# Latent attention: the query units of all eight token tiles first, then all value units, in place of one loop over both

## The reference, cut to what matters

```
def mla_attention(c_q, c_kv, k_rope, positions, q_norm_g, kv_norm_g, w_uq, w_ukv):
    q = (rmsnorm_2(c_q, q_norm_g) @ w_uq).reshape(B, S, MLA_HEADS, MLA_QK_DIM)          # 8 heads x 96
    q = jnp.concatenate([q[..., :MLA_NOPE_DIM], rope(q[..., MLA_NOPE_DIM:], positions)], axis=-1)
    q = q * (MLA_QK_DIM ** -0.5)
    kv = (rmsnorm_2(c_kv, kv_norm_g) @ w_ukv).reshape(B, S, MLA_HEADS, MLA_NOPE_DIM + MLA_V_DIM)
    k_nope, v = kv[..., :MLA_NOPE_DIM], kv[..., MLA_NOPE_DIM:]                           # 64 and 64 a head
    k_pe = rope(k_rope[:, :, None, :], positions)
    k = jnp.concatenate([k_nope, jnp.broadcast_to(k_pe, (B, S, MLA_HEADS, MLA_ROPE_DIM))], axis=-1)
    ...
        s = jnp.einsum('bqhd,bkhd->bhqk', q_blk, k).astype(jnp.float32)
        p = jax.nn.softmax(s, axis=-1).astype(v.dtype)
        return jnp.einsum('bhqk,bkhd->bqhd', p, v)
```

## Time and profile before

| | before |
|---|---|
| runs (median; lowest, highest) | 1961.69 us; 1956.64, 1961.73 |
| span of the profiled execution | 1955.4 us |
| median of the runs less that span | 6.3 us |
| PE busy | 1805.7 us (92%) |
| DVE, ACT, POOL busy | 869.1, 580.1, 470.5 us |
| mean granted TensorE clock | 0.964 |
| tile loop, first matmul to last value matmul | 1468.08 to about 1492.2 us |
| first matmul of the second key unit | 1496.52 us |

### The profile page before, as it was taken

How to read it: one execution, slowest core, us unless ns; L and a number is a source line. 1 busy time by engine, 2 the same in 40 slices (tenths; PEclk the granted TensorE clock), 3 DMA queues, 4 the chain that set the end, 5 groups by cost and what they waited for, 6 DMA issues and landing times. The chain is left out here.

```text
span 1955.4 us, 23181 instructions
## 1 busy us (share of the span) xinstructions
PE 1805.7 (92%) x9240; PEld 1540.5 (79%) x9240; DVE 869.1 (44%) x1393; ACT 580.1 (30%) x1320; POOL 470.5 (24%) x314
## 2 busy tenths in 40 slices
PE   4999899897999999999899999999997999968998
PEld 3777798676877768889898998877776888856776
DVE  4140577336502125521455305422325999963633
ACT  4101244124300114410243003411123776641111
POOL 5223300323322220202202121203321323230330
PEclk8999999898999999999999999999997999988999
DMA  6112200333322110101102011244443111124332
GB/s 195 28 65 66 64 1 1 114 121 114 102 86 70 44 44 17 60 12 44 45 21 61 19 42 44 66 139 134 135 159 113 30 33 31 25 92 145 124 119 86
DMA packets 85387, 142.44 MB, mean 73 GB/s; under 512 B 26656, under 2 KB 36512, under 8 KB 85152
## 3 DMA queue, kind: packets, MB, share of 16 engines
q10 hardware_dynamic: 55216, 84.46, 12.7%
q1 hardware_dynamic: 30064, 56.50, 9.7%
HBM read 102.20 MB, written 38.73 MB: 72 GB/s over the span
## 5 line engine op out<-in xcount | busy, mean ns | idle before, releaser
L495 POOL TENSOR_SCALAR w_hi<-w_stage 128x1024 fp32r<-128x1024 f32 (+4 forms) x123 | 129.2, 1054 | 1203.0 <-PEq L767 523.3
L499 POOL TENSOR_TENSOR w_lo<-w_stage,w_hi 128x1024 fp32r<-128x1024 f32 (+4 forms) x123 | 270.8, 2206 | 9.2
L762 PE MATMUL ps<-w_hi,h2T_hi 128*128 128x512 f32 x584 | 250.9, 430 | 2.3 <-issue 1.6
L762 PE MATMUL ps<-w_hi,h2T_lo 128*128 128x512 f32 x584 | 238.2, 408 | 0.0
L762 PE MATMUL ps<-w_lo,h2T_hi 128*128 128x512 f32 x584 | 237.9, 407 | 0.0
L1720 DVE TENSOR_TENSOR rope_cos_part<-ps,cos_dil 128x512 f32<-128x512 f32 x48 | 33.2, 692 | 374.7 <-PE ps L762 374.7
L762 PEld LDWEIGHTS ps<-w_hi,h2T_hi 128*128 128x128 f32 x584 | 161.2, 276 | 15.7 <-issue 5.1
L762 PEld LDWEIGHTS ps<-w_hi,h2T_lo 128*128 128x128 f32 x584 | 161.3, 276 | 10.5
L762 PEld LDWEIGHTS ps<-w_lo,h2T_hi 128*128 128x128 f32 x584 | 162.2, 278 | 9.3
L520 PE MATMUL ps<-h2T_hi,w_hi 128*128 128x512 f32 x384 | 156.0, 406 | 3.8 <-ACT gate_tiles L1207 2.4
L520 PE MATMUL ps<-h2T_lo,w_hi 128*128 128x512 f32 x384 | 153.9, 401 | 0.0
(11 more groups left out here) (265 smaller groups left out, 3583.5 us busy)
## 6 DMA issues: line engine op xcount, KB each, us to landing
w_stage<-in_w_in SPq DMA_DIRECT2D x76, 512.0 KB, 3.6
w_stage<-in_w_out SPq DMA_DIRECT2D x16, 512.0 KB, 3.6
gate_scr<-gate_tiles ACTq DMA_DIRECT2D x16, 512.0 KB, 2.9
gates<-gate_scr ACTq DMA_DIRECT2D x32, 256.0 KB, 2.7
dil_scr<-dil_out ACTq DMA_DIRECT2D x24, 264.0 KB, 2.1
dil_nums<-dil_scr ACTq DMA_DIRECT2D x24, 256.0 KB, 3.6
x_tiles<-in_x ACTq DMA_DIRECT2D x8, 512.0 KB, 8.7
x_back<-in_x ACTq DMA_DIRECT2D x8, 512.0 KB, 3.6
```

The lines of the kernel that those rows point to most:

```text
L495: last = nc.gpsimd.tensor_scalar(hi_, raw_, 1.0, 0.0, ALU.mult, ALU.add)
L499: last = nc.gpsimd.tensor_tensor(lo_, raw_, hi_.bitcast(F32), ALU.subtract)
L762: m = pe.matmul(ps[:, u % 2, :], toks(a, k), b[:, s, k, :], start=(k == 0 and b is wh and a is h2h), stop=(k == KT - 1 and a is h2l))
```

## The change

The loop over tiles is written as two on TensorE and on VectorE, and as three pieces on ScalarE: all query units with their spills, the last spill, then all value copies. Nothing is added or taken away: 96 query matmuls, 48 value matmuls, 16 query copies, 8 value copies, 8 ropes, 8 low parts and 8 spills as before, with the same waits between the same pieces. The buffers stay as they are.

```
 # TensorE
                 three_passes(ps[:, u % 4, 0:384], [ ... ]).then_inc(sem("qm_done"), 1)
+        for t in range(TT):
             if t >= 2:
                 pe.wait_ge(*after("vm_lo", t - 1))
             for n in range(2):
...
 # ScalarE
                                ACT.Copy, scale=float(MLA_QK) ** -0.5).then_inc(sem("qm_read"), 1)
-            act.wait_ge(*after("vm_done", t + 1))
-            act.activation(V2[:, t, :, 0, :], ps[:, 4 + t % 2, :].rearrange("p (h c) -> p h c", c=HD), ACT.Copy).then_inc(sem("vm_hi"), 1)
             if t >= 1:
                 act.wait_ge(*after("qm_roped", t))
                 act.dma_start(qm_d[P * (t - 1):P * t, :], q_sb[:, (t - 1) % 2].rearrange("p h c -> p (h c)")).then_inc(sem(f"qm_spill{(t - 1) % 2}"), 16)
+        act.wait_ge(*after("qm_roped", TT))
+        act.dma_start(qm_d[P * (TT - 1):, :], q_sb[:, (TT - 1) % 2].rearrange("p h c -> p (h c)")).then_inc(sem(f"qm_spill{(TT - 1) % 2}"), 16)
+        for t in range(TT):
+            act.wait_ge(*after("vm_done", t + 1))
+            act.activation(V2[:, t, :, 0, :], ps[:, 4 + t % 2, :].rearrange("p (h c) -> p h c", c=HD), ACT.Copy).then_inc(sem("vm_hi"), 1)
         for b in range(4):
             act.wait_ge(*after(f"g_spill{b}", 16 * 6))
-        act.wait_ge(*after("qm_roped", TT))
-        act.dma_start(qm_d[P * (TT - 1):, :], q_sb[:, (TT - 1) % 2].rearrange("p h c -> p (h c)")).then_inc(sem(f"qm_spill{(TT - 1) % 2}"), 16)
...
 # VectorE
             nc.vector.tensor_tensor(q_hi, q_t[:, 2], q_t[:, 3], ALU.add).then_inc(sem("qm_roped"), 1)
+        for t in range(TT):
             dve.wait_ge(*after("vm_hi", t + 1))
             nc.vector.tensor_tensor(V2[:, t, :, 1, :], ps[:, 4 + t % 2, :].rearrange("p (h c) -> p h c", c=HD),
```

## The result

The changed kernel takes 1969.50 us in the median of seven runs (1961.07 to 1976.24), beside 1959.72 for seven runs of the kernel before (1953.44 to 1962.06). The ratio is 1.0052, with a 95% interval from 1.0033 to 1.0071: slower by 10 us, between 6.5 and 14. It was predicted as 1969.1, slower by 7.4.

A forecast was written before the change was run, and what follows sets the result against it. The query spill loop and TensorE were taken to run side by side at 2.79 us a tile. Second key unit 8.1 us later, less 0.7 for its full clock, gave 7.4 on 1961.7: 1969.1 us, range 1963 to 1973.5.

The forecast's parts named there:

- The likeliest case: Tile loops: spill-paced queries, TensorE empty, two-bank value rounds, uncovered first key unit; 7.4 us slower, chance 0.55.
- Step 1, the pace: Query units: spill loop sets the pace, spills 2.4 and 2.9 us apart by turns, each issued 0.01 behind copies.
- the other end, 0.40: Query spills: issue 0.40 us behind the next tile's copies, pace stays 2.79, last spill only 0.9 us earlier.
- Step 1, the first spill: Tile 0's spill: issued at about 1474.6 where before it waited until 1475.49 behind the value copy.
- Step 2: Value units: TensorE without work for 6 us, then two-bank rounds of 2.9 us at half or 2.3 at full clock.
- Step 3: Way into head 0: nothing covers the first key unit; second key unit starts 8.1 us later, stage 7.4 slower.
- the 0.7 us that the second key unit was to give back: Second key unit: at full clock it takes 0.97 us in place of 1.66, returning 0.7.
- Half clock through all the value units: Rival, value units: half clock to their end, +10.0 us, 1971.7; chance 0.25 shared with later spill issue.
- the later issue: Rival, query spills: 0.40 us issue delay on top of half clock, +10.9 us, 1972.6; within the shared chance 0.25.
- the clock pays back: Rival, head 0: full clock from 1498 to 1512 cuts the loss to +2.4 us, 1964.1; chance 0.12.
- A stretch after 1512 that differs by more than a microsecond: Sign of being wrong, after the stage: a difference of over a microsecond beyond the shift.
- the queries run at TensorE's own pace: Rival, query units: 2.08 us a tile, last spill 4.1 us earlier, +3.3 us, 1965.0; chance 0.05.

The follow-up runs named there:

- e7_before_load: Kernel before, old order, with eight-tile room in `q_tok` and head 0's query load issued between the two key copies: ratio 1.0007 against the kernel before.
- e4_warm: Changed kernel with 44 idle matmuls into an unused bank between value units 1 and 2: ratio 1.0031 against the kernel before.
- e1_banks: Changed kernel with the eight value units spread over seven banks in place of two: ratio 0.9999 against the kernel before.
- e5_early_load: Changed kernel with head 0's query load issued between the value copies of tiles 2 and 3: ratio 1.0030 against the kernel before.
- e2_slots: Changed kernel with room for eight query tiles in `q_tok` in place of two: ratio 1.0020 against the kernel before.
- e6_before_slots: Kernel before, old order, with room for eight query tiles in `q_tok` in place of two: ratio 0.9993 against the kernel before.
- e8_combined: Changed kernel with eight-tile `q_tok`, seven value banks, and first key unit, its copies, last spill and head 0's load moved: ratio 0.9963 against the kernel before.

## Why the prediction was right, and where its terms were off

**The way it went.** The likeliest case was the one that came: spill loop, empty TensorE, rounds over two banks, and a key unit that nothing covers. The stage lost 8.95 us where the sum had 7.4. By its steps, in us from the first query matmul:

- **Step 1, the pace.** Spills were to be 2.4 and 2.9 apart by turns; behind the first they are 2.4 and 2.8. The choice of 0.01 for the issue behind the copies was right (0.05 to 0.07 measured); the other end, 0.40, is excluded by these rows. The Trainium skill's "Perfetto Trace Analysis", "Sequencer Loop", has the sequencer hand an engine instruction to a queue and go on to the next; the trace agrees for one waiting copy (0.05 us).
- **Step 1, the first spill.** This is the first term that was mis-sized, by 0.77. It was to land 2.31 after its issue and took 3.08. That puts tile 2's copies 0.7 late and, through the turns of the loop, the last spill 0.5 (25.46 for 24.9). For the same reason TensorE's waits for copies begin with tile 4 and not with tile 6. The first two spills, from issue to landing:

```profile
1477.60 3.08 DMA qmla_scr<-q_tok
...
1480.81 2.31 DMA qmla_scr<-q_tok
```

What else the DMA engines moved meanwhile is in the list of queues (packets, MB, share of the 16 engines). In the changed kernel, from 1477.6 to 1480.7:

```profile
q10 hardware_dynamic: 144, 0.39, 33.3%
q8 instruction: 1, 0.02, 2.1%
q1 hardware_dynamic: 17, 0.02, 1.7%
```

And before, from 1475.5 to 1477.8:

```profile
q10 hardware_dynamic: 144, 0.39, 43.9%
```

Queue 10 is the spill, 16 times nine packets. Queue 1 is SP's, with the weights of the output projection; its last packet ends 0.28 us after the issue, and the spill's first starts 0.83 after it, so the weights were out of the way. Queue 8 is one packet of 16 KB of the program's own instructions. It takes about 1 us, and behind it the last packets of the spill run one after another, 0.12 us apart, when all the others have ended. I read this as one engine that comes late by that packet; the spill lands with its last. The packets of other runs say the same (us from the spill's issue; the first column of numbers is the issue itself, from the first query matmul):

| kernel | issued | instruction packet | last packet of the spill | landed |
|---|---|---|---|---|
| before | 7.41 | -0.71 to 0.23 | 1.96 | 2.31 |
| e7_before_load | 7.22 | -0.75 to 0.52 | 1.97 | 2.33 |
| changed | 6.49 | 0.23 to 1.26 | 2.58 | 3.08 |
| e4_warm | 6.48 | 0.46 to 1.38 | 2.71 | 3.18 |
| e1_banks | 6.06 | 0.67 to 1.59 | 2.91 | 3.39 |
| e5_early_load | 6.83 | 0.66 to 2.13 | 3.46 | 3.93 |

In the last four the spill's last packet comes 1.32 to 1.33 us after the end of the instruction packet. In e5_early_load the weights had ended before the issue, and it was the slowest. In these runs the instruction packet starts 6.5 to 7.5 us into the stage, with either order. So the earlier issue won nothing, because it ran into a transfer that it had been behind. I had not asked what the earlier spill would meet. No run takes the packet away or moves it, so this rests on the times of the packets.
- **Step 2.** TensorE was to stand for 6 us and stood for 5.5. The rounds were taken as 2.9 and 2.3 and are 3.06 at half clock and 2.4 to 2.6 at full clock; value unit 7 ended 7.7 us after unit 2's start, where I had 7.4. The first matmul after a wait takes 0.1 to 0.2 longer than the next ones. The clock was back about 3.5 us after work began again (1498.32 to some 1501.8), where I had chosen 4.
- **Step 3.** From the first key unit to the second 2.44, as at full clock (2.5 with the drain in front of it). But the 0.7 us that the second key unit was to give back did not come: it ran at half clock, 1.61 us. The clock fell near 1508.7, just after a wait of 1.48 us, with gaps of up to 0.33 us between the value units before it. This is the second term that was mis-sized. I had counted on full clock because of the work before, and hadn't put the wait beside it. In e4_warm the same unit ran at full clock after the same 1.48 us, in e2_slots at half; what decides it stays open.

In sum, the first spill is 0.5 at the last spill, the value rounds 0.3 and the key unit 0.7, together 1.5; 8.95 less 7.4 is 1.55.

**The rivals.** Half clock through all the value units did not happen, nor did the later issue. That the clock pays back is excluded the other way: head 0 started at half clock in both kernels. In the changed one it lasted until after 1529, so that the fourth query tile's scores came 10.6 us after the first and not 8.5. That is the 2 us lost inside head 0. A stretch after 1512 that differs by more than a microsecond was a sign that I had named for being wrong, and it came. But the order doesn't decide it: the same stretch takes 10.4 and 10.5 us in e6_before_slots and e7_before_load, which have the old order, and 8.5 in e4_warm and e8_combined, which have the new one. It is about 8.5 or a little over 10 with either order, by one profile of each kernel; whether the new order makes the longer one more frequent isn't shown. That the queries run at TensorE's own pace is excluded by e2_slots: they do only when the spills are out of the way.

**The size.** The time was met by 0.4 us, which is luck in part: the runs of before had a lower median this time (1959.7 for 1961.7), and the slowdown was larger by as much. The chances leaned on a forecast that lay only 1.5 us beyond what can be told from no change; a forecast of the 8.95 us that the stage lost would have lain 3 us beyond.

## What to carry to other kernels

When two loops of equal pace run side by side, splitting one out saves nothing until the other's limit is lifted too: give the loop that stays its buffers and the one that moves its banks before reordering, and then move up what the new order lets go early. Without that last step the order broke even here. With two buffers, a unit waits for nothing only if its round through the engines is no longer than the time from one unit to the next but one: here a round of 2.3 to 2.4 us against 2 x 2.79 in the old order, and against two units of 0.7 in the new one. And when a transfer is issued sooner, look at what the DMA engines carry at that new time, the program's own instructions included.

## What the runs showed of the hardware

- A transfer on ScalarE's queue is issued while one activation is running and one is waiting (0.05 to 0.07 us after the first copy starts), but not with two waiting: in the old order, with a value copy behind the two query copies, it was 0.40, the start of the second copy.
- A packet of 16 KB of instructions (0.9 to 1.5 us) that started 0.2 to 0.7 us after a spill's issue held up one sixteenth of the spill and so its landing: 3.08 to 3.93 us in place of 2.31.
- TensorE's clock fell to 1.2 GHz about 2.2 us into a complete wait (work ended at 1492.8, fall near 1495.0), but also near 1508.7, just after a wait of only 1.48 us. In e2_slots it stayed at 2.4 GHz through a wait of 2.84 us. In e2_slots and e4_warm the second key unit had the same 1.48 us of waiting before it, and before that value units at full clock with gaps of 0.70; it ran at half clock in the one and at full clock in the other.
- Identical code ahead of the stage reached it anywhere from 1466.7 to 1477.9 us in eleven profiles whose stage starts with queries. For a change of 9 us in 1960, the distance between two points of one trace says more than the span.
